# Page numbers of a paged cache read eight at a time into registers, in a one-core decoder step

## What is computed

```
past = kv_pages[page_table]            # 8 sequences x 64 pages x 128 rows, 4 groups of 128 numbers
full = concatenate([past, new row])
kc, vc = compress(full[:, :, 0]), compress(full[:, :, 1])

def compress(kv, pe, w1, w2):          # blocks of 32 rows, every 16 rows
    pieces = kv.reshape(b, n_c + 1, 16, heads, 64)
    hid = sum(einsum('bncgd,cdf->bngf', pieces[:, p:p + n_c] + pe[p], w1[p]) for p in (0, 1))
    return einsum('bngf,fd->bngd', gelu(hid), w2)
```

## Time and profile before

| | |
|---|---|
| median of 3 runs | 3990.92 us (3977.38 to 3991.05) |
| profiled execution | 3991.6 us, of which the span of the trace is 3989.7 us |
| TensorE busy, of the span | 3406.4 us (85%) |
| GpSimd busy, of the span | 529.6 us (13%) |
| granted TensorE clock, mean of the span | 0.871 |
| page transfers | 384 on SyncE's queue, 640 on GpSimd's, 64 KB each |

### The profile page before, as it was taken

How to read it: one execution, slowest core, us unless ns; L and a number is a source line. 1 busy time by engine, 2 the same in 40 slices (tenths; PEclk the granted TensorE clock), 3 DMA queues, 4 the chain that set the end, 5 groups by cost and what they waited for, 6 DMA issues and landing times. The chain is left out here.

```text
span 3989.7 us, 52799 instructions
## 1 busy us (share of the span) xinstructions
PE 3406.4 (85%) x17868; PEld 2874.1 (72%) x17868; DVE 1380.8 (35%) x3147; ACT 858.3 (22%) x1541; POOL 529.6 (13%) x820
## 2 busy tenths in 40 slices
PE   2999999999978964596999953579998499999996
PEld 2888888888855553464777731279888499999996
DVE  3233232323241046101555540121113444444445
ACT  1233332323221012001344410011111311111112
POOL 4233333333200000000000016600000000000000
PEclk9899898989898966697888875559999799999998
DMA  8657675767432000503000012231103211111111
GB/s 138 101 94 110 94 109 91 110 94 107 62 133 87 0 1 3 175 6 134 11 11 6 6 44 85 85 85 39 41 26 112 90 53 42 50 44 47 47 32 43
DMA packets 300187, 263.82 MB, mean 66 GB/s; under 512 B 48938, under 2 KB 269598, under 8 KB 299080
## 3 DMA queue, kind: packets, MB, share of 16 engines
q1 hardware_dynamic: 188814, 159.88, 15.7%
q0 software_dynamic: 37376, 59.36, 7.4%
q10 hardware_dynamic: 73786, 42.18, 6.8%
HBM read 232.71 MB, written 32.48 MB: 66 GB/s over the span
## 5 line engine op out<-in xcount | busy, mean ns | idle before, releaser
L168 POOL DMA_DIRECT2D raw<-in_cache_nsa_kv x640 | 380.8, 595 | 661.8 <-issue 661.8
L2013 PE MATMUL bank<-xH,cwH 128*128 128x512 f32 x1024 | 425.1, 415 | 0.0
L2013 PE MATMUL bank<-xL,cwH 128*128 128x512 f32 x1024 | 413.6, 404 | 0.0
L2013 PE MATMUL bank<-xH,cwL 128*128 128x512 f32 x1024 | 411.4, 402 | 0.0
L2013 PE MATMUL bank<-u2H,fwiH 128*128 128x344 f32 x1056 | 338.2, 320 | 38.4 <-DVE fwiL L2389 38.4
L2013 PE MATMUL bank<-u2H,fwiL 128*128 128x344 f32 x1056 | 337.8, 320 | 0.0
L2013 PE MATMUL bank<-u2L,fwiH 128*128 128x344 f32 x1056 | 337.6, 320 | 0.0
L374 DVE COPY x<-bank 64x512 f32<-64x512 f32 x256 | 175.9, 687 | 417.8 <-PE bank L280 415.6
L472 ACT ACTIVATE x<-bank 64x512 f32<-64x512 f32 x256 | 151.4, 591 | 739.6 <-PE bank L280 612.4
L380 DVE TENSOR_TENSOR xL<-x,xH 128x1024 fp32r<-128x1024 f32 x128 | 157.0, 1227 | 240.0 <-ACT xH L481 240.0
L2013 PEld LDWEIGHTS bank<-xH,cwL 128*128 128x128 f32 x1024 | 198.6, 194 | 47.2
(11 more groups left out here) (448 smaller groups left out, 5837.9 us busy)
## 6 DMA issues: line engine op xcount, KB each, us to landing
raw<-in_cache_nsa_kv POOLq DMA_DIRECT2D x640, 64.0 KB, 4.6
raw<-in_cache_nsa_kv SPq DMA_DIRECT2D x384, 64.0 KB
wada<-in_w_ada ACTq DMA_DIRECT2D x48, 512.0 KB, 14.7
fwi<-in_w_ffn_in SPq DMA_DIRECT2D x44, 512.0 KB, 4.1
fwo<-in_w_ffn_out SPq DMA_DIRECT2D x22, 512.0 KB
gwg<-in_w_in SPq DMA_DIRECT2D x20, 512.0 KB, 4.0
wada<-in_w_ada_final ACTq DMA_DIRECT2D x16, 512.0 KB, 17.8
mw<-in_w_in SPq DMA_DIRECT2D x3, 2048.0 KB, 9.8
```

What stands on the lines that cost most here:

```text
L168: eng.dma_start(k.raw[8 * q:8 * q + 8, kv, nt], pages[bass.ds(at, 1), :, :, P * kv:P * kv + P] .rearrange("o n s c -> (o n) s c")).then_in ...
L2013: mm = pe.matmul(out, a[x], b[y], start=start and n == 0, stop=stop and n == 2)
```

## The change

`load_page` goes. `load_pages` now goes through its pages in groups of eight: one call loads eight numbers of the table into eight registers of the queue that issues (with the same range), and then eight transfers are issued. The engine's name is a new argument, `which`, and the four call sites on each queue pass it. Pages, sizes, destinations, semaphores and the split stay.

```
-    nt, q = page // 16, page % 16
-    at = eng.value_load(k.pt[0:1, bass.ds(i * NPAGES + page, 1)], min_val=0, max_val=POOL - 1)
-    eng.dma_start(k.raw[8 * q:8 * q + 8, kv, nt], pages[bass.ds(at, 1), :, :, P * kv:P * kv + P]
-                  .rearrange("o n s c -> (o n) s c")).then_inc(sems[kv][nt], 16)
...
-    for page in range(lo, hi):
-        load_page(k, eng, i, page, kv, sems)
+    for page in range(lo, hi, 8):
+        _, at = k.nc.values_load_multi_w_load_instructions(k.pt[0:1, bass.ds(i * NPAGES + page, 8)], engines=[which],
+                                                           min_val=0, max_val=POOL - 1)
+        for q in range(8):
+            nt, p0 = page // 16, 8 * (page % 16 + q)
+            eng.dma_start(k.raw[p0:p0 + 8, kv, nt], pages[bass.ds(at[q], 1), :, :, P * kv:P * kv + P]
+                          .rearrange("o n s c -> (o n) s c")).then_inc(sems[kv][nt], 16)
...
-                    load_pages(k, sp, i, kv, 0, SPLIT, k.s_page)
+                    load_pages(k, sp, mybir.EngineType.SP, i, kv, 0, SPLIT, k.s_page)
...
-                    load_pages(k, pool, i, kv, SPLIT, NPAGES, k.s_pagep)
+                    load_pages(k, pool, mybir.EngineType.Pool, i, kv, SPLIT, NPAGES, k.s_pagep)
```

More of the change, by code:

```diff
@@ L160, in shared_buffers, with load_pages @@
     k.smalltok_d = k.dram("smalltok_d", (B, 32))
-def load_page(k, eng, i, page, kv, sems):
-    nt, q = page // 16, page % 16
+def load_pages(k, eng, which, i, kv, lo, hi, sems):
+    k.nc.disable_value_cache = True
     pages = k.i["cache_nsa_kv"][0].rearrange("q (n s) v g d -> q n s (v g d)", s=STRIDE)
-    at = eng.value_load(k.pt[0:1, bass.ds(i * NPAGES + page, 1)], min_val=0, max_val=POOL - 1)
-    eng.dma_start(k.raw[8 * q:8 * q + 8, kv, nt], pages[bass.ds(at, 1), :, :, P * kv:P * kv + P]
-                  .rearrange("o n s c -> (o n) s c")).then_inc(sems[kv][nt], 16)
-def load_pages(k, eng, i, kv, lo, hi, sems):
-    k.nc.disable_value_cache = True
-    for page in range(lo, hi):
-        load_page(k, eng, i, page, kv, sems)
+    for page in range(lo, hi, 8):
[5 more added lines that the diff above has]
+                          .rearrange("o n s c -> (o n) s c")).then_inc(sems[kv][nt], 16)
     k.nc.disable_value_cache = False
@@ L241, in _ @@
             sp.wait_ge(k.s_pt, 16)
-            load_pages(k, sp, 0, 0, 0, SPLIT, k.s_page)
-            load_pages(k, sp, 0, 1, 0, SPLIT, k.s_page)
+            load_pages(k, sp, mybir.EngineType.SP, 0, 0, 0, SPLIT, k.s_page)
+            load_pages(k, sp, mybir.EngineType.SP, 0, 1, 0, SPLIT, k.s_page)
             with sp.Fori(1, B) as i:
@@ L258, in _ @@
             pool.wait_ge(k.s_pt, 16)
-            load_pages(k, pool, 0, 0, SPLIT, NPAGES, k.s_pagep)
-            load_pages(k, pool, 0, 1, SPLIT, NPAGES, k.s_pagep)
+            load_pages(k, pool, mybir.EngineType.Pool, 0, 0, SPLIT, NPAGES, k.s_pagep)
+            load_pages(k, pool, mybir.EngineType.Pool, 0, 1, SPLIT, NPAGES, k.s_pagep)
             with pool.Fori(1, B) as i:
```

## The result

| | median us (lowest to highest) | ratio to the kernel before [95% interval] |
|---|---|---|
| before, same comparison | 3984.15 (3973.1 to 3991.05) | |
| changed | 4098.01 (4083.97 to 4106.86) | 1.0285 [1.0244, 1.0327] |
| forecast | 3981 (3968 to 3997) | |

The forecast had the wrong sign. The profiled execution of the changed kernel took 4083.97 us, the lowest of its four; its span is 4082.3. Lines moved up by three: 277 is the transpose, 469 ScalarE's copy, 168 the loads, 172 the page transfers, 181 the modulation weights.

What follows compares the result with a forecast made beforehand. TensorE was taken to bound the steady state, with page transfers mattering only where it waits in three places: -4 (start) - 7.5 (ScalarE's copies) + 1 (second item) = -10.5, from 3991.6 to 3981 us, range 3968 to 3997.

Steps and rivals of the forecast that it cites:

- Issue: Page issue on both queues: SyncE from 2.11 to 1.42 us a page, GpSimd from 1.25 to about 1.0.
- the sum for SyncE: SyncE's issue at the start: 1.42 us a page left, so twenty-four pages take 34 us in place of 50.
- Place one: The start, where TensorE waits for the first item's 64 pages: a gain of 4 us, bounds 12 and -2.
- the ten pages left: SyncE's queue after 45 us at the start: 8 to 9 us to drain, and 2 more to land.
- Place two: TensorE's waits behind ScalarE's copies from 134 us on: both gone, -4.7, with the clock -7.5; bounds -7.5 and 0.
- ScalarE's two bursts meet a nearly free DMA: Within an item: SyncE's page issue ends at 30, GpSimd's at 40 us, leaving ScalarE's modulation weights and store room.
- Place three: The second item's 2.18 us wait for modulation weights at 155.63 us: faster pages compete, +1, bounds 0 and 8.
- C: Rival, chance 0.08: denser page bursts crowd out what ScalarE asks for, in the second item; slower, 4002 us.
- 37 us in, behind most of the pages: Argument against crowding in later items: each asks for its modulation weights 37 us in, behind most of the pages.
- A: Rival, chance 0.25: transfers, not their issue, are the limit at the start and in ScalarE's queue; -1, 3990 us.
- B: Rival, chance 0.13: the start is bound by issue after all; -11 - 7.5 + 1, 3974 us.

## Why the prediction was wrong, point by point

- *Issue.* Right in its prices: 1.08 and 0.58 us a load of eight, against 1.1 and 0.6, and GpSimd's pace of 0.97 us a page against 1.0. For SyncE's load that was luck: I took its 0.79 us as mostly the way there and back, paid once. With pages on 16 partitions a single load takes 0.27 and a load of eight 0.54, so most of the 0.79 hung on the pages in front of it. Each further register cost 0.04 us on GpSimd (0.58 for eight, 0.29 for one). The Trainium skill, "Runtime: NRT & Kernel Launch", section "Instruction fetch mechanics", gives about 200 ns a register even in bulk, by which eight would take 1.6 us (an estimate from that page). The runs show less. The step that failed is the sum for SyncE: I took the 0.76 us of a transfer's own issue as fixed. In the changed kernel single issues took up to 12.1 us, and the 24 pages were issued by 77.5 us and not by 37.
- *Place one.* The failed step is the drain: "the ten pages left" at 0.9 to 1.1 us. That rate came from the last 7 us before the transposes; the 15 us from 45 to 60 give 1.3, with the weights nearly done and GpSimd's pages landing 5.9 us after their issue. In the changed kernel these land after 13.3 us, 0.56 MB of weights stand beside them from 45 to 70 us, and a page of SyncE took 7 us. I named one side of this as the lower bound (GpSimd takes more than SyncE gains) and gave it 2 us; the start cost 37.5. The other side I did not name: SyncE's own faster pages, with GpSimd at its old pace, already cost 31.7. A warning stood in the earlier trace rows: SyncE's sixteenth page was 18 us in the queue, and from 45 us on, while it still waited, the share was 0.72. I read a low share as room. With 16 partitions 29 of 31 pages issued by 45 us had been moved (1.90 MB), where it was 14 of 20: I now read it as room that pages on 8 partitions could not use.
- *Place two.* Wrong in sign: not -7.5 but +71. The failed step is "ScalarE's two bursts meet a nearly free DMA". I counted when pages are issued (until 30 and 40 us after an item's first transposes) and not when they have landed. ScalarE's weights, 36 us in, met pages that had been issued and not landed. Its queue moved 1.18 MB in the 14.8 us of such an issue, where it had moved 1.78, and yet the DMA as a whole was not fuller: 0.97 of its share against 1.18. The run with ScalarE's issues 13 us later shows that the meeting is the whole of the loss in the items.
- *Place three.* The wait for modulation weights that I priced at +1 to +8 is gone in the changed kernel (none is listed), so this rival's place was wrong. ScalarE now issues these weights at 165.56 us, 2 us ahead of GpSimd's first page (167.58); before, both went at 128 us. That this is the reason is not shown.
- *Rivals.* C had the right mechanism, pages crowding out what ScalarE asks for, but at one item and 10 us; it acts in every item, and through ScalarE's queue rather than through late weights. My reason against it ("37 us in, behind most of the pages") held for the pages' issue and not for their landing. A was right that issue was not the limit and wrong that nothing would move. B would have needed the spread: with 16 partitions and single loads GpSimd's fortieth page is issued at 51.05 us and the last wait ends at 53.71, so issue sets the start. With eight at a time that page is issued at 40.38, and the wait ends only at 50.74.
- *Range and chances.* I put 0.04 on slower by over 0.5%. The range had no term for queues that take each other's room.

## What to carry to other kernels

Before making an issue faster, ask whether the queue behind it drains faster than it is filled, with every other queue at its new pace too; a transfer that stands in its queue while the DMA share is 0.7, as here from 45 us on, may be one that cannot use what is free. Look then at how many partitions a transfer's destination has. And an engine that computes and also issues transfers, like ScalarE here, can be late with its computing while transfers of others are on their way, so put its issues where those have landed.

## What was not expected of the hardware

- From 20 to 45 us, beside the weights, the DMA moved 123 GB/s with 64 KB pages on 8 partitions, and 195 with the same bytes in the same 512-byte pieces on 16, at shares of 1.12 and 1.15.
- Beside GpSimd's pages and ScalarE's weights SyncE's queue moved a 64 KB page in 7 us; without either, in 0.6 us.
- An issue of SyncE took up to 12.1 us, and two small ones of ScalarE 29 us together, while earlier transfers of their queues were waiting.
- A register load of SyncE took 0.79 us behind pages on 8 partitions and 0.27 behind pages on 16.
